# The last 16 up chunks of each layer in two halves of 256 tokens, in an encoder with product-key experts

## What is computed

```python
def peer(h, w_q, sub_keys, u_tab, v_tab):
    ...
    def block(args):
        xb, ib, gb = args
        a = jnp.einsum("tmd,td->tm", u_tab[ib], xb)
        wgt = gb * jax.nn.gelu(a, approximate=False)
        return jnp.einsum("tm,tmd->td", wgt, v_tab[ib])
```

## Time and profile before

| | before |
|---|---|
| median of 3 runs | 3185.29 us |
| lowest, highest | 3184.82, 3186.6 us |
| span of the profiled execution | 3183.3 us |
| TensorE matmul busy | 3087.5 us, 97% of the span |
| VectorE, GpSimd, ScalarE busy | 2460.2, 1200.7, 1118.5 us |
| mean granted TensorE clock | 0.988 |

### The profile page before, as it was taken

The page is one execution under the profiler, slowest core; times in us unless marked ns, Lnnn a source line. Parts: engine busy times, 40 slices in busy tenths (PEclk is TensorE's granted clock), DMA queues, the critical chain, the costliest instruction groups (busy, mean ns, idle before and its releaser), DMA issues.

```text
span 3183.3 us, 55078 instructions
## 1 busy us (share of the span) xinstructions
PE 3087.5 (97%) x16200; PEld 2681.0 (84%) x16200; DVE 2460.2 (77%) x5952; ACT 1118.5 (35%) x1590; POOL 1200.7 (38%) x765
## 2 busy tenths in 40 slices
PE   6989999999999999999999999999999999999998
PEld 4668888878888999999975788888788889999997
DVE  7981999959995488999877239951799927889997
ACT  3333322324343333333343332223334423333333
POOL 0033445420001366777700334444000024667674
PEclk8999999999999999999999999999999999999999
DMA  6162666445556799999921224444455578999996
GB/s 256 60 217 101 241 231 241 170 140 198 207 210 251 255 362 360 360 358 370 371 90 39 86 83 144 145 146 141 159 209 212 186 290 286 362 357 362 360 375 240
DMA packets 328654, 734.74 MB, mean 231 GB/s; under 512 B 37088, under 2 KB 168544, under 8 KB 326624
## 3 DMA queue, kind: packets, MB, share of 16 engines
q1 hardware_dynamic: 236864, 462.04, 42.2%
q0 software_dynamic: 50688, 151.18, 12.9%
q10 hardware_dynamic: 40992, 120.34, 9.7%
HBM read 613.85 MB, written 119.54 MB: 230 GB/s over the span
## 4 chain that ended last, share of the span: by engine, by line
PE 54%; POOL 18%; issue 13%; DVE 10%; DMA 2%; ACTq 1%; ACT 1%; DVEq 0%; SPq 0%; POOLq 0%
PE bank L499 30%; PE bank L503 15%; POOL z_pad L926 9%; POOL u_pad L920 5%; PE bank L608 3%; POOL z_pad L920 2%; POOL scratch L920 2%; PE bank L520 2%; DVE scratch L1277 2%; PE bank L419 1%; ACTq L818 1%; DVE h L1255 1%; DVE h L1258 1%; PE bank L443 1%; DMA scratch<-g_scratch 1%
## 5 line engine op out<-in xcount | busy, mean ns | idle before, releaser
L499 PE MATMUL bank<-h_hi,w_hi 128*128 128x512 f32 x2528 | 996.6, 394 | 18.0 <-ACT norm_tmp L799 15.1
L665 ACT ACTIVATE w_hi<-ring 128x1024 fp32r<-128x1024 f32 x584 | 614.9, 1053 | 1112.0 <-PE bank L503 1034.6
L499 PE MATMUL bank<-h_lo,w_hi 128*128 128x512 f32 x2528 | 986.9, 390 | 0.0
L905 POOL TENSOR_TENSOR w_lo<-ring,w_hi 128x1024 fp32r<-128x1024 f32 x172 | 446.1, 2595 | 836.3 <-ACT w_hi L665 836.2
L625 PE MATMUL bank<-v_lo,w_hi 128*128 128x368 f32 x2032 | 670.0, 330 | 0.0
L625 PE MATMUL bank<-v_hi,w_hi 128*128 128x368 f32 x2032 | 665.4, 327 | 2.2 <-DVE v_lo L1423 2.2
L503 PE MATMUL bank<-h_hi,w_lo 128*128 128x512 f32 x2528 | 624.3, 389 | 0.0
L499 PEld LDWEIGHTS bank<-h_hi,w_hi 128*128 128x128 f32 x2528 | 476.1, 188 | 117.8 <-ACT w_hi L665 17.9
L499 PEld LDWEIGHTS bank<-h_lo,w_hi 128*128 128x128 f32 x2528 | 476.0, 188 | 96.9
L503 PEld LDWEIGHTS bank<-h_hi,w_lo 128*128 128x128 f32 x2528 | 474.6, 188 | 98.5
L926 POOL DMA_INDIRECT z_pad<-ga_scratch,z_pad x288 | 374.1, 1299 | 155.3 <-issue 86.5
(11 more groups left out here) (183 smaller groups left out, 2886.8 us busy)
## 6 DMA issues: line engine op xcount, KB each, us to landing
ring<-u_t SPq DMA_DIRECT2D x256, 512.0 KB, 3.4
ring<-v_t SPq DMA_DIRECT2D x256, 512.0 KB, 6.8
ga_scratch<-norm_tmp ACTq DMA_DIRECT2D x256, 256.0 KB, 2.0
g_scratch<-scratch ACTq DMA_DIRECT2D x12, 4096.0 KB, 13.8
scratch<-ga_scratch SPq DMA_DIRECT2D x256, 192.0 KB, 6.7
scratch<-g_scratch SPq DMA_DIRECT2D x128, 384.0 KB, 6.8
scratch<-ada_t SPq DMA_DIRECT2D x76, 512.0 KB, 5.8
ring<-wq_t SPq DMA_DIRECT2D x32, 512.0 KB, 3.4
```

Source lines behind the costliest of these rows:

```text
L499: pe.matmul(to, w_hi[:, b, k * P:(k + 1) * P], part_h[:, k, :], start=(k == 0 and part_h is h_hi), stop=False)
L665: return act.activation(to, of, ACT.Copy)
L905: pool.tensor_tensor(w_lo[:, n % 2, :], ring[:, n % RING, :], w_hi[:, n % 2, :].bitcast(F32), ALU.subtract).then_inc(tile_used[n % RING], 1)
```

## The change

The last 16 chunks of each layer's up stage (the loop that was at L611) are multiplied by `up_halves` in place of `up_chunk`. It takes tokens 0 to 255 through all 24 matmuls into bank 0 or 1, increments a new semaphore `half_done`, then takes tokens 256 to 511 through all 24 again, into bank 6 or 7. So it issues 48 matmuls of 256 columns, each with its own load of the weights. On ScalarE `gelu_halves` activates the first half when `half_done` says so, ahead of `hi`, and the second half behind `hi`; the store is one DMA as before. Since the second halves now lie in banks 6 and 7, the first down chunk waits for the last Gelu before k = 6 in place of k = 0. The number of stores, tile loads and splits is unchanged.

```diff
@@ -242,7 +242,7 @@
         split_hi, chunk_done, gelu_done = sem("split_hi"), sem("chunk_done"), sem("gelu_done")
         ga_stored = [sem(f"ga_stored{s}") for s in range(RING)]
         retrieved, exp_done, gate_ready = sem("retrieved"), sem("exp_done"), sem("gate_ready")
-        turned = sem("turned")
+        turned, half_done = sem("turned"), sem("half_done")
         hot_ready, gate_product, gate_copied = sem("hot_ready"), sem("gate_product"), sem("gate_copied")
         g_stored = [sem(f"g_stored{b}") for b in range(2)]
         ga_landed = [sem(f"ga_landed{s}") for s in range(RING)]
@@ -608,9 +608,30 @@
                                 mm = pe.matmul(to, hot2[:, b, j, :], hot1[:, b, j, q, :], start=(q == 0), stop=(q == 1))
                         mm.then_inc(gate_product, 1)
 
+                def up_halves(r, s):
+
+                    b = s % 2
+                    pe.wait_ge(gelu_done, N_U * l + RING * r + s + 1)
+                    wait_hi(pe, l, r, stages["u"] + s)
+                    for half in range(2):
+                        cols = slice(half * T // 2, (half + 1) * T // 2)
+                        to = bank[:, 6 * half + b, 0:T // 2]
+                        for k in range(KC):
+                            for part_h in (h_hi, h_lo):
+                                pe.matmul(to, w_hi[:, b, k * P:(k + 1) * P], part_h[:, k, cols],
+                                          start=(k == 0 and part_h is h_hi), stop=False)
+                        if half == 0:
+                            wait_lo(pe, l, r, stages["u"] + s)
+                        for k in range(KC):
+                            mm = pe.matmul(to, w_lo[:, b, k * P:(k + 1) * P], h_hi[:, k, cols],
+                                           start=False, stop=(k == KC - 1))
+                        if half == 0:
+                            mm.then_inc(half_done, 1)
+                    mm.then_inc(chunk_done, 1)
+
                 with pe.Fori((EARLY + LATE) // RING, N_U // RING) as r:
                     for s in range(RING):
-                        up_chunk(r, s)
+                        up_halves(r, s)
 
 
                 def down_chunk(r, s, first=False):
@@ -618,7 +639,7 @@
                     wait_hi(pe, l, r, stages["v"] + s)
                     pe.wait_ge(w_ready, N_V * l + RING * r + (s + 1 + RING))
                     for k in list(range(2, KC)) + [0, 1]:
-                        if first and k == 0:
+                        if first and k == 6:
 
                             pe.wait_ge(gelu_done, N_U * l + N_U + 2)
                         for part_w in (v_hi, v_lo):
@@ -842,10 +863,21 @@
                 with act.Fori(0, GBLOCKS // 2) as pair:
                     for b in range(2):
                         gate_block(pair, b)
+                TAIL = N_U - EARLY - LATE
+
+                def gelu_halves(r, s):
+
+                    act.wait_ge(ga_stored[s], 16 * (N_U // RING) * l + 16 * r + 16)
+                    act.wait_ge(half_done, TAIL * l + RING * r + (s + 1 - EARLY - LATE))
+                    act.activation(norm_tmp[:, s, 0:T // 2], bank[:, s % 2, 0:T // 2], ACT.Gelu)
+                    hi(r, stages["u"] + s + 2)
+                    act.activation(norm_tmp[:, s, T // 2:T], bank[:, 6 + s % 2, 0:T // 2], ACT.Gelu).then_inc(gelu_done, 1)
+                    act.wait_ge(gelu_done, N_U * l + RING * r + (s + 3))
+                    act.dma_start(ga_dram[RING * r + s], norm_tmp[:, s, :]).then_inc(ga_stored[s], 16)
+
                 with act.Fori((EARLY + LATE) // RING, N_U // RING - 1) as r:
                     for s in range(RING):
-                        hi(r, stages["u"] + s + 2)
-                        gelu(r, s)
+                        gelu_halves(r, s)
 
                 def split_v(r, n):
 
@@ -858,8 +890,7 @@
                     if s >= 2:
                         act.wait_ge(w_step, N_V * l + (s - 1))
                         copy(v_hi[:, s - 2, 0:TD], ga_in[:, s - 2, 0:TD]).then_inc(v_high, 1)
-                    hi(N_U // RING - 1, stages["u"] + s + 2)
-                    gelu(N_U // RING - 1, s)
+                    gelu_halves(N_U // RING - 1, s)
 
                 def high_rounds(start, end):
                     with act.Fori(start, end) as r:
```

## The result

| | before | changed |
|---|---|---|
| median | 3185.29 us (5 runs) | 3196.51 us (5 runs) |
| lowest, highest | 3184.82, 3190.44 us | 3194.54, 3202.62 us |
| span of the profiled execution | 3183.3 us | 3192.9 us |
| mean granted TensorE clock | 0.988 | 0.989 |

The ratio is 1.0032, with a 95% interval from 1.0022 to 1.0043: the change makes the kernel slower, by 11.2 us in the medians and by 7 to 14 us within the interval. I had forecast 3195.9 us and a growth of 10.6. Two single executions took far longer than all others of their kernel, 11009.82 us in experiment 5 and 3473.89 us in experiment 7; they stand in no ratio, and move those two medians by at most 0.2 us.

A forecast was written before the change was run, and what follows sets the result against it. TensorE's matmuls were taken to bound the kernel, filling 97% of the span. Added to the 3185.3 us median, +10.2 us for the halved matmuls and +0.4 us for the moved wait gave 3195.9 us, range 3190 to 3204.

The forecast's parts named there:

- TensorE alone bounds the last up chunks: Last 16 up chunks per layer: TensorE is busy for all 87.14 us and alone sets the time.
- The Gelu's overlap brings nothing: Last up chunks: an earlier Gelu gains nothing, since its bank is wanted only 3.85 us after it ends.
- 13.3 ns fixed per matmul: Last up chunks: 24 more matmuls each cost 13.3 ns, 0.32 us per chunk, +10.2 us in all.
- A weight load needs some 110 ns and is just hidden: Last up chunks: a weight load takes some 110 ns, 10 less than the 120 ns distance of 256-column matmuls.
- The upper bound: Last up chunks: 13.3 ns on top of a 110 ns load, 123.3 ns per matmul, +15.4 us in all.
- the second rival: Last up chunks: the weight load adds to the fixed part, 123 to 130 ns per matmul, 3201.1 to 3211 us; chance 0.17.
- The third rival: Last up chunks: the weight load's whole 188 ns count, up to 9.02 us per chunk, +115 us; chance 0.03.
- The first rival: Last up chunks: only 2.7 ns fixed per matmul at 256 columns, 2.1 us in all, 3187.8 us; chance 0.10.
- The moved wait: First down chunk: waiting for the last Gelu behind 8 matmuls, not 12, idles TensorE 0.2 us per layer, +0.4 us.
- Nothing downstream absorbs it: Down stage and layer ends: the delay reaches the end; later waits for own rows, 4.3 us, hide none of it.

The follow-up runs named there:

- experiment 5: Changed kernel with the first down chunks reordered, so the wait for the last Gelu stands behind 12 matmuls again: 3195.59 us, ratio 1.0028 to the kernel before.
- experiment 7: Kernel before, unsplit, with each layer's last down chunk doing its 24 matmuls ahead of the wait for the own rows: 3180.11 us, ratio 0.9977.
- experiment 2: Kernel before with only the Gelu of the last 16 up chunks cut in two, TensorE multiplying whole chunks: 3188.77 us, ratio 0.9998.
- experiment 1: Kernel before with only TensorE's part: last 16 up chunks as 48 matmuls of 256 columns in one bank; 3199.19 us, ratio 1.0031.
- experiments 3 and 4: 3: changed kernel in quarters of 128 columns, 3358.08 us; 4: experiment 1 cut at token 320 into 320 and 192 columns, 3213.67 us.
- experiment 6: Kernel before with experiment 1's halves for all 128 up chunks of a layer in place of the last 16: 3263.87 us in one run.

## Why the prediction was right, step by step

- *TensorE alone bounds the last up chunks.* Right: the windows grew by what its matmuls grew by, and experiment 2 left the time alone.
- *The Gelu's overlap brings nothing.* Right: experiment 1 has no overlap, and its window of 16 chunks is as long as the changed kernel's.
- *13.3 ns fixed per matmul, the same at 256 columns as at 368 and 512.* Right: 120.0 ns, 5.76 us per chunk, 5.09 us per layer, +10.2 us. The two points of the earlier trace rows were enough, and a third and fourth at 256 and 320 columns lie on their line. That the median came within 0.6 us of the forecast is partly luck, since the growth is known only to 7 to 14 us; the windows are what bears the term out.
- *A weight load needs some 110 ns and is just hidden.* Right, and now measured at 111.7. The upper bound, the fixed part on top of the load, was the second rival at 0.17; the 120.0 ns and experiments 3 and 4 refute it. The third rival, the records' full 188 ns, falls with them.
- *The first rival, a fixed part of 2.7 ns as in f32.* Wrong for this format, as the 120.0 ns show. By the rule of the Trainium skill (TensorE: Matmul & The Clock Gate, Back-to-back issue gap) 256 columns would be an estimated 109 ns apart. The trace disagrees, with 120.0. The same page of the Trainium skill (LDWEIGHTS) gives a load the columns of the weight divided by 1.2, an estimated 107 ns for 128. Experiment 3's loads follow at 111.7 ns, some 5 more, while their records last 0.19 us.
- *The moved wait, 0.2 us per layer.* The mechanism was right and the size too small: 0.35, of which the end of the kernel may see less (experiment 5). I had expected it in the list of TensorE's waits, where only the weight loads have it. I had taken a half Gelu at 0.33 us (it is 0.36 to 0.37) and counted only the gap, not the slower start of the matmul behind it, 0.27 us in place of 0.167.
- *Nothing downstream absorbs it.* Right for the 10.2 us: the own rows come later with the up stage, and were waited for 4.9 us as against 4.3. I had not thought of the half clock behind that wait, which moves a single execution by 1.5 us.

## What to carry to other kernels

Cutting a matmul along its columns to start the consumer sooner pays only where the producer waits for that consumer; ask first who waits for whom, and by how much the slack is short. Its price is read from the trace before it is made: two widths of the same instruction give the fixed part, and the closest pair of weight loads gives the floor under it. Here that price was 13.3 ns for each further matmul, and below some 237 columns it would have been steep, 5 us per chunk more at 128 columns than at 256. Look for the gain where TensorE waits, and put independent matmuls ahead of the wait: that gave 7 us here, about half of it by the clock.

## What was not expected of the hardware

- The floor under the distance of matmuls is sharp: 111.7 ns at 128 columns and 111 at 192, with matmuls at 320 on the line of the columns to half a nanosecond.
- The f32r matmuls have a fixed part of 13.3 ns, records of f32 one of 2.7 ns. Where the difference comes from was not tried and stays open.
- Behind matmuls of f16 the first 16 of a chunk cost 0.10 us more at 512 columns and 0.04 at 256 (experiment 6).
- A wait of 2.2 us ahead of the last down chunk is followed by a stretch at half clock in some executions (0.89 on the mean of 15.8 us) and not in others (1.00 in both layers of experiment 5).
